# Own homes and own banks for the last plain unit ahead of the seven-product units, in a two-layer decoder kernel

## The reference

```
D_MODEL = 1024;  D_FF = 2816
def swiglu(x, w13, w2):
    gate, up = jnp.split(x @ w13, 2, axis=-1)
    return (jax.nn.silu(gate) * up) @ w2
x = layer_norm(ALPHA * x + 0.5 * swiglu(x, w13, w2), g, b)
```

## Time and profile before

| | us |
|---|---|
| median of 3 runs | 2198.03 (2197.64 to 2198.89) |
| profiled execution | 2195.15 |
| its span | 2193.5 |
| PE busy | 2086.8 (95%) |
| DVE busy | 1421.7 (65%) |
| ACT busy | 867.4 (40%) |
| mean granted TensorE clock | 0.976 of full speed |

### The profile page before, as it was taken

The page is one execution under the profiler, slowest core; times in us unless marked ns, Lnnn a source line. Parts: engine busy times, 40 slices in busy tenths (PEclk is TensorE's granted clock), DMA queues, the critical chain, the costliest instruction groups (busy, mean ns, idle before and its releaser), DMA issues.

```text
span 2193.5 us, 43507 instructions
## 1 busy us (share of the span) xinstructions
PE 2086.8 (95%) x16575; PEld 2014.1 (92%) x16575; DVE 1421.7 (65%) x2358; ACT 867.4 (40%) x1529; POOL 228.8 (10%) x267
## 2 busy tenths in 40 slices
PE   7999999999999999999999999999978789999998
PEld 7999999999999999999999999998965588999997
DVE  3583895685795597389549835267645377828955
ACT  3341453353453254254325525222234345514533
...
DMA packets 381501, 249.80 MB, mean 114 GB/s; under 512 B 10422, under 2 KB 363038, under 8 KB 381326
## 3 DMA queue, kind: packets, MB, share of 16 engines
...
## 4 chain that ended last, share of the span: by engine, by line
PE 73%; DVE 11%; DMA 6%; issue 4%; ACT 3%; SPq 1%; POOL 1%; DVEq 0%; ACTq 0%; POOLq 0%
PE pair L762 33%; PE pair L894 27%; PE pair L801 5%; DMA t_w_raw<-in_attn_w_kv 3%; PE pair L1022 2%; DMA t_w_raw<-in_ffn_w 2%; DVE t_w_seven L1984 2%; DVE t_w_lo L1862 1%; PE pair L1271 1%; DVE t_w_sum L1979 1%; PE pair L774 1%; DVE t_u_sum L2265 1%; ACT t_w_hi L1400 1%; DVE t_stream L2190 1%; DVE t_u L1988 1%
## 5 line engine op out<-in xcount | busy, mean ns | idle before, releaser
L894 PE MATMUL pair<-t_x_diff_hi,t_w_seven 128*128 128x272 f32 x1960 | 409.9, 289 | 0.0
L1862 DVE TENSOR_TENSOR t_w_lo<-t_w_raw,t_w_hi 128x1024 fp32r<-128x1024 f32 (+2 forms) x152 | 233.0, 1533 | 200.0 <-ACT t_w_hi L1400 194.6
L1400 ACT ACTIVATE t_w_hi<-t_w_raw 128x1024 fp32r<-128x1024 f32 (+2 forms) x152 | 177.3, 1171 | 446.7 <-PE pair L762 374.2
L894 PEld LDWEIGHTS pair<-t_x_diff_hi,t_w_seven 128*128 128x128 f32 x1960 | 320.3, 188 | 0.0
L762 PE MATMUL pair<-t_h_lo,t_w_hi 128*128 128x272 f32 x1232 | 254.8, 288 | 0.0
L762 PE MATMUL pair<-t_h_hi,t_w_lo 128*128 128x272 f32 x1232 | 254.6, 288 | 0.0
L762 PE MATMUL pair<-t_h_hi,t_w_hi 128*128 128x272 f32 x1232 | 254.5, 288 | 0.0
L894 PE MATMUL pair<-t_x_hi,t_w_seven 128*128 128x272 f32 x1120 | 240.7, 295 | 11.2 <-DVE t_c L1988 9.9
L894 PE MATMUL pair<-t_x_diff_lo,t_w_seven 128*128 128x272 f32 x840 | 241.7, 288 | 0.0
L894 PEld LDWEIGHTS pair<-t_x_hi,t_w_seven 128*128 128x128 f32 x1120 | 184.5, 188 | 23.4 <-issue 12.5
L762 PEld LDWEIGHTS pair<-t_h_hi,t_w_lo 128*128 128x128 f32 x1232 | 193.2, 188 | 0.0
...
## 6 DMA issues: line engine op xcount, KB each, us to landing
...
```

What stands on the lines that cost most here:

```text
L894: m = nc.tensor.matmul(out[:, 0:HALF], w[:, k, :], b, start=start and k == 0 and j == 0, stop=k == 3 and j == 2, skip_group_check=not start)
L1400: nc.scalar.activation(whi[s][:, 0:KT[stage], :], raw[s][:, 0:KT[stage], :], ACT.Copy) \
L1862: nc.vector.tensor_tensor(wlo[s][:, 0:k, :], raw[s][:, 0:k, :], whi[s][:, 0:k, :].bitcast(F32), ALU.subtract).then_inc(lo_made[s], 1)
```

## The change

`weights(stage, s, i)` now tells where the rounded weights of a unit lie. The last plain unit of `up<f>a` (`apart` and `aside`) gets four tiles of its own, laid over parts of `h_hi` and `h_lo` that are written only later; its results go to bank pairs `pc` and `pd`. Its rounding on ACT and DVE stands one unit's step sooner, ahead of the silu of the unit before it, and waits only for the products of unit 1 (`USED + 2`). ACT's first four shifts go ahead of that silu, its four `x_diffs_hi` behind it; DVE's `hidden` of that unit stands behind the four `x_diff_lo`. The ring's parts wait for the last but one plain unit only, so that all of `seven_high` 0 to 5 and `seven_low` 0 to 5 stand ahead of the last unit's `hidden`. PE's one wait ahead of the first seven-product unit is divided over its products 0, 1, 2 and 5.

In `down<f>a` the last unit's second pair of weights (s = 1) gets its own home, laid over the elementwise tiles and the small sums; its two results go to `pc` and `pd`; its rounding and the additions to `x` are taken out of the loop. Again the ring's parts wait for less, and PE's wait for `part_made` is divided over products 0, 1, 2 and 5.

```diff
+def aside(stage, i):
+    return isinstance(i, int) and i == PLAIN[stage] - 1
+
+def apart(stage, i):
+    return isinstance(i, int) and (stage[:2] == "up" and i == PLAIN[stage] - 1 or
+                                   stage[:4] == "down" and stage[5] == "a" and i == UNITS[stage] - 1)
...
+        whi_down = sb(rq, "w_hi_last_down", [P, KH, P], F32R)
+        wlo_down = sb(rk, "w_lo_last_down", [P, KH, P], F32R)
+        sb(rh, "before_last_up", [P, 8 * 4 * HALF + 5 * T])
+        whi_up = [sb(rh, f"w_hi_last_up{s}", [P, DC, P], F32R) for s in range(2)]
+        wlo_up = [sb(rh, "w_lo_last_up0", [P, DC, P], F32R)]
+        sb(rh, "between_last_up", [P, KH * T - 3 * DC * P])
+        wlo_up += [sb(rh, "w_lo_last_up1", [P, DC, P], F32R)]
...
@@ tensor, pair() @@
                 if first and stage[3] == "a":
-                    pe.wait_ge(gate_silu, GATED[stage] + PLAIN[stage])
-                    pe.wait_ge(h_made, HIDDEN[stage] + PLAIN[stage])
+                    pe.wait_ge(gate_silu, GATED[stage] + PLAIN[stage] - 1)
                 elif first:
-                    pe.wait_ge(part_made, DC * (f + 1))
+                    pe.wait_ge(part_made, DC * (f + 1) - 3)
...
@@ tensor, up(), turn(i) @@
+                    gate_out, up_out = (pc, pd) if aside(stage, i) else (pa, pb)
-                        pe.wait_ge(gate_silu, gated + reused(stage, i))
-                    products(pa, 0, DC, stream_x, stream_xl).then_inc(w_used[0], 1)
+                        pe.wait_ge(gate_silu, gated + (2 if aside(stage, i) and normed else reused(stage, i)))
+                    products(gate_out, 0, DC, stream_x, stream_xl, own=weights(stage, 0, i)).then_inc(w_used[0], 1)
...
@@ tensor, linear() @@
-                with pe.Fori(3 if normed else 1, UNITS[stage] - (stage in RES)) as i:
+                with pe.Fori(3 if normed else 1, UNITS[stage] - (stage in RES or spare)) as i:
                     turn(i, False)
+                if spare:
+                    pe.wait_ge(c_made, 5 * SEVEN[stage])
+                    for s in range(2):
+                        pe.wait_ge(lo_made[s], base + UNITS[stage])
+                        products(ps[2 + s], s, KT[stage], hi, lo, own=weights(stage, s, UNITS[stage] - 1)) \
+                            .then_inc(w_used[s], 1)
@@ scalar, round_hi() @@
+                if second(stage, i) or apart(stage, i) and stage[:2] == "up":
                     for n in range(2):
-                        act.wait_ge(w_used[n], USED[stage])
+                        act.wait_ge(w_used[n], USED[stage] + (2 if apart(stage, i) else 0))
...
+                if apart(stage, i) and s == 1:
+                    act.wait_ge(h_lo_made, HIDDEN["up" + stage[4:]] + KH)
+                    nc.scalar.activation(whi_down[:], raw[s][:], ACT.Copy).then_inc(hi_made[s], 1)
@@ scalar, seven_high() @@
-                    act.wait_ge(w_used[0 if n < 3 else 1], USED[stage] + PLAIN[stage])
+                    act.wait_ge(w_used[0], USED[stage] + (PLAIN[stage] - 1 if stage[3] == "a" else 0))
+                    act.wait_ge(w_used[1], USED[stage] + PLAIN[stage] - 1)
@@ scalar, up() @@
+                    if i == n - 2:
+                        round_hi(nxt, 0, j)
+                        round_hi(nxt, 1, j)
+                        if stage in NORMED:
+                            act.wait_ge(t_made, 4 * f + 4)
+                            add_shift(stage, 0)
+                        silu(stage, i)
+                        x_diffs_hi(f)
+                        hidden_hi(stage, i)
+                        if stage in NORMED:
+                            add_shift(stage, 1)
+                        continue
...
-                seven_high(0, y, stage)
+                for m in (0, 1, 2):
+                    seven_high(m, y, stage)
                 silu(stage, n - 1)
-                for m in (1, 2, 3):
+                for m in (3, 4, 5):
                     seven_high(m, y, stage)
@@ vector, up() @@
+                    if i == n - 2:
+                        round_lo(nxt, 1, j)
+                        for m in range(4):
+                            x_diff_lo(f, m)
+                        hidden(stage, i)
+                        hidden_lo(stage, i)
+                        continue
...
-                seven_low(0, y)
-                seven_low(1, y)
-                seven_low(2, y)
+                for m in range(6):
+                    seven_low(m, y)
                 hidden(stage, n - 1)
-                seven_low(3, y)
                 hidden_lo(stage, n - 1)
-                seven_low(4, y)
-                seven_low(5, y)
@@ vector, down_first() @@
                 add_part(0, UNITS[stage] - 1)
-                seven_low(1, y)
-                seven_low(2, y)
+                for n in range(1, 6):
+                    seven_low(n, y)
                 add_part(1, UNITS[stage] - 1)
-                for n in (3, 4, 5):
-                    seven_low(n, y)
```

81 lines of the change are left out of this document (48 added, 33 removed).

## The result

The changed kernel takes 2161.43 us (median of 4 runs, 2159.01 to 2166.71), the kernel before beside it 2197.84 (4 runs, 2195.77 to 2198.89): a ratio of 0.9842, 95% interval 0.9826 to 0.9858. The profiled execution took 2159.01 against 2195.15 before, so 36.1 less.

The account below looks back on a forecast made before the run. PE bounds the kernel, busy 2086.8 of 2193.5 us; only its idle time can shrink. Terms 9.5 + 4.1 + 3.7 + 3.3 + (7.3 - 0.4) + 1.3 = 28.8, say 29, from 2198.03 give 2169; range 2163.5 to 2179 with rivals.

Parts of the forecast that it names:

- Last plain units and joints of `up1a` to `up3a`: Three waits behind t_w_lo go, 9.5 us; waits for the last unit's silu at the first seven-product units go too.
- the clock term: Last plain units of up1a and up3a: slow clock after the 3.2 us gaps goes, 2.6 + 1.5 = 4.1 us.
- each wait counted here sits on the chain that ended last, so what goes shifts the end one to one: PE's stages run one behind the other, so each us of counted wait removed ends the kernel one us earlier.
- Product 6: PE's t_c waits in seven-product units: first units' 7.3 us go but 0.4; half of later units' 2.6, 1.3, goes.
- the 0.5 to 2 us forecast: Sign in the changed kernel's profile that the forecast was right: PE's waits behind t_c at 0.5 to 2 us.
- `up0a`'s joint: PE's wait for the last unit's silu before up0a's first seven-product unit goes; part of 3.7 us in four a stages.
- against so much play: Three runs within 1.25 us were taken to speak against slow stretches varying enough to make the sum 25 to 33.
- the rival in which the clock moves elsewhere: Slow stretches at the norms fall otherwise, each costing or giving 1.5 to 2.6 us: 2165 or 2173; chance 0.10.
- The rival in which DVE becomes the bound: DVE has hardly a free place, so waits behind t_c stay: gain 20.8 us, 2177.3; chance 0.17.
- the one in which ACT is blocked by a load: In up<f>a the earlier silu stands behind roundings awaiting raw; with loads 12 us late, 2201, slower; chance 0.02.

Follow-up runs that it names:

- wait_one: Changed kernel with PE's waits for the last unit's silu and hidden, or last add_part in down<f>a, together ahead of product 0 again; 2174.73 us, ratio 0.9907.

## Why the prediction missed

The mechanisms held, and no rival came true as told. What failed is the size of the terms: first the price of a wait, which the forecast put at its idle time alone. By terms, from the table of stages:

**Last plain units and joints of `up1a` to `up3a`** (9.5 + 2.6 forecast of idle time, 4.1 of clock; 17.6 measured on the mean). The gaps went as worked out. The clock's part is 17.6 less 12.1 less 1.0 (next point), 4.5, against 4.1. Some 0.6 of it is the stretch at the norm of `up1a`, which one of three traces before and one of four after have; so the clock term was right on the mean, and by some luck, since it was read from one trace and the next two have other stretches. The first pair of traces has more, since in the first trace of before 13.7 us of slow clock lay in `up1a`'s stage and in the first of after none.

**A wait was priced at its idle time.** That is the step that failed for the waits, in "each wait counted here sits on the chain that ended last, so what goes shifts the end one to one". A matmul in steady work starts 0.125 us behind the last one and lasts 0.29, so 0.165 us of the next is hidden under it; idle time is counted from the modelled end, and the 0.165 is lost as well. The matmul behind a wait is also slow to hand over: the next starts 0.23 behind it and not 0.13, so a wait costs a further 0.1. The joint behind `down1a` shows it: the stage from its first matmul to the first of `up1b` is 67.35 us before and 66.35 after, 1.00 less where the wait was 0.82.

First matmuls of `down1a` and `up1b`, before:

```profile
681.05 0.41 PE L762 MATMUL pair<-t_h_hi,t_w_hi 128*128 128x272 f32 x2
...
748.40 0.40 PE L894 MATMUL pair<-t_x_hi,t_a_hi 128*128 128x272 f32 x1 [0.82 <-DVE t_stream L2105]
748.63 0.29 PE L894 MATMUL pair<-t_x_lo,t_a_hi 128*128 128x272 f32 x1
```

after:

```profile
665.41 0.41 PE L795 MATMUL pair<-t_h_hi,t_w_hi 128*128 128x272 f32 x2
...
731.76 0.29 PE L927 MATMUL pair<-t_x_hi,t_a_hi 128*128 128x272 f32 x1
731.89 0.29 PE L927 MATMUL pair<-t_x_lo,t_a_hi 128*128 128x272 f32 x1
```

and wait_one, where the unit is out of the loop as in the changed kernel and only the wait is back:

```profile
672.90 0.42 PE L795 MATMUL pair<-t_h_hi,t_w_hi 128*128 128x272 f32 x2
...
740.24 0.39 PE L927 MATMUL pair<-t_x_hi,t_a_hi 128*128 128x272 f32 x1 [0.82 <-DVE t_stream L2155]
```

That is 67.34: the 0.17 belongs to the wait and not to the loop's branch. In the `a` joints of wait_one 1.87 of idle time cost 2.04. The Trainium skill has both parts of the overlap (page "TensorE: Matmul & The Clock Gate", sections "Single matmul latency" and "Back-to-back issue gap"): its formulas for full clock, the first given for bf16, put a matmul of 272 columns at an estimated 0.28 us and the start of the next at 0.116 behind it, an estimated overlap of 0.163. The trace agrees on the overlap; its 0.125 from start to start is 8% more. For the ten waits of the plain units and joints the overlap is 1.7 us.

**Product 6** (6.9 + 1.3 forecast, 10.1 measured in the seven-product stages). The `t_c` waits did not fall to the 0.5 to 2 us forecast: the list of PE's waits has 3.9, 1.9, 3.6 and 3.5 in the four traces after, against 9.9, 11.7 and 10.3 before, 7.4 less. In the first unit of each `a` stage `t_c` still comes 0.3 to 0.6 late, and not 0.1; only in `up1a` of the first trace is it 0.9, where ACT's second high part waited 0.45 us for its load and all behind it on ACT and DVE shifted by as much. The 0.3 that is always there is the overlap once more: the forecast let PE end units at their busy time, 12.19 us, where the next one starts after 12.03, so PE is at product 0 of `up1a` 18.1 us after `hidden_hi` of unit 1 and not 18.4 (570.84 to 588.96 after; 579.14 to 597.57 in the forecast), while DVE's chain held. In the first units of the `b` stages no wait is left. Yet 2.7 more came in than the idle time. That is about what the other costs of a wait give: 0.165 + 0.1 for each of eight waits for `t_c` that are gone, and the 0.1 behind each of the eight joints, 2.9 together.

**`up0a`'s joint** (1.1): gone in every trace, and invisible in the stage's length, since that ranges over 4 us with the slow stretches in it.

**Kv and attention, taken as constant** (0 forecast): 2.5 on the mean of the traces, over a range of 9 within one and the same kernel. The change removed no wait there, and what makes these stages longer or shorter from one execution to the next stays open.

Together 28.8 forecast, less 1.1 for `up0a`, plus 1.7 for overlaps in joints, 1.9 at product 6, 0.4 of clock, 2.5 in attention: 34.2 against 34.0 measured between the means of the traces. The medians are 2 to 4 us further apart still, and no trace shows where. Between 28.8 and the 36.4 of the result lie 7.6 us. The price of a wait explains 4.4 of them (1.7 in the joints, 2.7 at product 6); less idle time at product 6 (7.4 for 8.2) and `up0a` took back 1.9; and 4.9, kv and attention and what the traces miss, are not explained. The range was too narrow for a second reason: the three runs shown lay within 1.25 us, and the forecast took that as evidence "against so much play". In the later comparisons the same kernel spread from 2189 to 2205.

Of the rival in which the clock moves elsewhere, the first pair of traces has the stretch at the norm of `up1a` gone, but the gain is as large by the later medians. The rival in which DVE becomes the bound was partly true: `t_c` is what PE now waits for in the first units of `up1a` to `up3a`, for 0.4 to 0.9 us and not 1.1 to 1.4. Of the one in which ACT is blocked by a load the 0.45 us are the start, far from the 4 from which it decides; in all four traces there is no wait of PE behind `t_w_lo` in these stages.
